# Six of twelve modulation weight tiles: multiplied by TensorE in column quarters instead of by VectorE

## The chip, the cores and the metric

The kernel runs on one core of one Trainium2 chip, in one launch. The metric is device time in microseconds (us). TensorE (PE) multiplies and writes only to PSUM; VectorE (DVE) and ScalarE (ACT) do elementwise work and may read PSUM; GpSimd (POOL) does some elementwise work and issues indirect gathers; SyncE (SP) issues the large weight transfers. The engines run side by side and meet only at semaphores.

## The reference, cut to what matters

256 tokens of width 1024 pass through two transformer-like blocks. The first block is modulated by a condition vector c, and this is the part that the change touches:

```
c_act = silu(c)                                    # (1, 1024)
mod = (c_act @ ada_w + ada_b)[:, None, :]          # (1, 6144)
sh1, sc1, gt1, sh2, sc2, gt2 = split(mod, 6)
h = rms_norm(x, g) * (1 + sc1) + sh1
p = h @ w_in                                       # four mixers (rwkv7, spatial gating, short conv, S5) and gates
x = x + gt1 * (merged @ w_o)
h = rms_norm(x, g2) * (1 + sc2) + sh2
x = x + gt2 * (square(relu(h @ ffn_w1)) @ ffn_w2)
```

The second block has two attentions and a layer that gathers 128 expert rows for each token from a table in HBM. Everything is float32.

## The kernel before, in words

**The modulation.** `ada_w` is 1024 x 6144. It arrives as twelve tiles, ada 0 to 11, of 128 partitions x 4096 values (2 MB): eight chunks k of 128 input rows lie side by side, each 512 output columns wide. Tiles 0 to 3 make sh1 and sc1, which the first product needs; 4 and 5 make gt1; 6 to 9 make sh2 and sc2; 10 and 11 make gt2.

In VectorE's `ada_sum(i)` each of 128 partitions multiplies its eight chunks by its eight values of c_act (columns 0 to 7 of `cact`) and adds them up: two TENSOR_SCALAR (line 1177), six SCALAR_TENSOR_TENSOR (line 1180) into two accumulators, and one TENSOR_TENSOR that adds the two (line 1183). The result, 128 x 512, lies in `mrow[:, i % 2, :]`. The sum over the 128 partitions is left to TensorE: `mod_gt(i)` (line 547) multiplies `mrow` by a matrix of ones, `mod_T(i)` (line 540) multiplies by one column of ones, to have the result as a column. VectorE then adds the bias. Tile 2 is already shared: VectorE takes half of its chunks, TensorE the others with one column of c as weights (line 558).

**The order of the work.** Each engine's program is written out by hand, as a Python function per engine. For the mixers, all of them walk through the same generator, `mixer_order()`: projections, then a plan of gate tiles and modulation tiles. It is `PLAN = [gates 4, ada 4, gates 5, gates 2, ada 5, gates 3, bc 0, gates 6, gates 7, ada 6, gates 0, ada 7, gates 1]`, and ada 8 is put in the middle of gates 1. Between the halves of a gate product stand steps of the mixers' own chains (a table `SCHEDULE` of the letters a, b, c, d). So in a gate tile's time TensorE alternates four instructions of the gate (`gate`, line 613, eight in the profile) with short products of the rwkv7 chain "a" and the S5 chain "d" (mostly through a helper, line 517). VectorE's S5 levels are lines 1444 and 1451, its part of the rwkv chain lines 1525 to 1548. When the walk yields "ada", only VectorE does something; when it yields "mod", TensorE and VectorE do.

**Ada 9** stands behind the walk. On VectorE it is between the end of chain "d" and the end of chain "a"; TensorE's `mod_T(9)` stands behind `merge(0)`, ahead of the products `glu(1, 0)`, `glu(1, 1)` and `w_o`.

**The ring.** SyncE loads the tiles in one order (`STREAM`) into a ring of three places. A load waits until the tile that lay in its place is spent: for a tile of TensorE that is the semaphore of the bank with its last product, for an ada tile VectorE's count `ada_taken`. The place of ada 9 is next given to the first tile of `w_o`; that of ada 4 to ada 5, of ada 5 to o_c.

**PSUM.** Eight banks. Names from the pool "misc" take banks 4, 5, 6 in turn; to take a bank TensorE waits until its last content was drained.

Of the kernel before, what the change touches and what calls it, by code (L numbers as in the profile page):

```python
# [14 lines left out]
P = 128  # L15
# [261 lines left out]
def build(nc, A, out):  # L277
    with ExitStack() as ctx:
# [19 lines left out]
        cact = sb("cact", [P, 16])  # L298
        wf = sb("wf", [P, 8, 8])
# [188 lines left out]
        spent = {("ada", i): (sig("ada_taken"), i + 1 if i < 2 else i) for i in range(12) if i != 2}  # L488

        def summed(i):  # L490

            return sig("ada"), i + 1 if i < 2 else i
# [5 lines left out]
        def tensor():  # L498
# [49 lines left out]


# [276 lines left out]
            for what, arg in mixer_order():  # L826
                if what == "p":
                    project(*arg)
                elif what == "gate":
                    gate(*arg)  # L830
                elif what == "merge":
                    merge(*arg)
                elif what == "mod":
                    mod_gt(arg[0]) if arg[0] < 6 else mod_T(arg[0])
                elif what == "step":
                    next(branch[arg[0]], None)
                elif what == "rest":
                    for _ in branch[arg[0]]:
                        pass
# [33 lines left out]
            merge(0, "misc")  # L873
            mod_T(9)
# [260 lines left out]
        def vector():  # L1135
# [98 lines left out]
            tell(v.tensor_tensor(cact[:, 0:8], cols[:, C_C:C_C + 8], cact[:, 8:16], ALU.mult), "c_times")  # L1234
            after()
# [6 lines left out]
            ada_sum(2)  # L1242
            mod_T(0, 0)
# [358 lines left out]
            for what, arg in mixer_order():  # L1602
                if what == "p":
                    project(*arg)
                elif what == "merge":
                    merge(*arg)
                elif what == "ada":
                    ada_sum(*arg)
                elif what == "mod":
                    mod_gt(arg[0], 0, arg[0] - 4) if arg[0] < 6 else mod_T(arg[0], 4 * arg[0] - 8)  # L1610
                elif what == "step":
                    next(branch[arg[0]], None)
                elif what == "rest":
                    for _ in branch[arg[0]]:
                        pass
# [3 lines left out]
            ada_sum(9)  # L1619
# [354 lines left out]
        def scalar():  # L1974
# [221 lines left out]

            branch = {"a": rwkv(), "b": gating(), "c": iter(()), "d": s5()}
            for what, arg in mixer_order():
                if what == "p":
                    project(*arg)  # L2200
                elif what == "gate":
                    gate(*arg)
                elif what == "step":
# [19 lines left out]
            evacuate("zA", f4(zA))  # L2223
            glu(1, 0)
# [469 lines left out]
```

## Time and profile before

| what | us |
|---|---|
| median of 3 runs | 1472.91 (1471.83 to 1474.8) |
| span of the profiled execution, first to last instruction | 1467.3 |
| median less that span (what lies around it) | 5.6 |
| PE busy in the span | 1211.4 (83%) |
| DVE busy | 942.2 (64%) |
| ACT busy | 397.3 (27%) |
| POOL busy | 374.9 (26%) |

The profiled execution has its span and no total of its own, so the total is taken as the span and 5.6 us. The profile's page shows one execution. Its strips cut the span in 40 slices of 36.7 us; a digit is the busy share in tenths. Matmuls overlap, so the duration of one (601 ns for 128x512) is longer than the distance between the starts of two; the length of a group of many is the better measure. A float32 product of the code appears as two MATMUL rows, each with its weight load (PEld): "x8" in the profile is four products of the code.

### The profile page before, as it was taken

How to read it: one execution, taken by the hardware profiler on the slowest of the kernel's cores; microseconds unless marked ns; L12 is line 12 of the kernel's file. 1: busy time of each engine (PE TensorE's matmuls, PEld its weight loads, DVE VectorE, ACT ScalarE, POOL GpSimd, SP SyncE). 2: the span in 40 equal slices, each digit the busy share in tenths (PEclk: the TensorE clock that was granted, in tenths of full speed). 3: DMA queues.
4: the chain of work that ended last, by engine and by line, in shares of the span. 5: the costliest groups of instructions: out<-in, count | busy, mean ns of one | idle time of the engine just before them, and what ended most of it. 6: DMA issues, size and time to landing. Idle time of an engine off the chain costs nothing.

```text
span 1467.3 us, 14350 instructions
## 1 busy us (share of the span) xinstructions
PE 1211.4 (83%) x4968; PEld 748.5 (51%) x4968; DVE 942.2 (64%) x2039; ACT 397.3 (27%) x1051; POOL 374.9 (26%) x285
## 2 busy tenths in 40 slices
PE   4989999999999999888787377668589887787776
PEld 3875655664767775487553265333473333232322
DVE  6288877973210231175866799996788776776654
ACT  2242111131101222122201223333234333333323
POOL 0001211201000000022533243432358444444420
PEclk9999999999999999999989699988799999999999
DMA  9733434465896667479999999999999999999996
GB/s 396 270 122 129 140 129 176 173 229 229 293 358 280 239 235 245 177 321 424 423 424 423 423 422 421 425 421 422 384 400 421 420 421 420 421 420 421 420 421 265
DMA packets 56376, 484.31 MB, mean 330 GB/s; under 512 B 6512, under 2 KB 8816, under 8 KB 10224
## 3 DMA queue, kind: packets, MB, share of 16 engines
q0 software_dynamic: 36864, 268.45, 44.2%
q1 hardware_dynamic: 18288, 211.35, 36.9%
q10 hardware_dynamic: 1152, 3.59, 0.6%
q8 instruction: 39, 0.64, 0.2%
q14 instruction: 33, 0.27, 0.1%
HBM read 482.33 MB, written 1.05 MB: 329 GB/s over the span
## 4 chain that ended last, share of the span: by engine, by line
PE 45%; DMA 28%; DVE 19%; issue 4%; ACT 3%; POOL 0%; DVEq 0%; SPq 0%; ACTq 0%
PE ps L517 23%; DMA ring<-in_euv,arena 16%; DMA arena<-in_euv,arena 7%; PE ps L613 6%; PE ps L980 6%; PE ps L904 5%; DVE xr L1910 4%; DMA ring<-in_w 3%; DVE arena L1886 3%; PE ps L1115 3%; DVE arena L1444 1%; DVE ring L1886 1%; DVE arena L1451 1%; DMA ring<-in_pq 1%; DVE arena L1180 1%
## 5 line engine op out<-in xcount | busy, mean ns | idle before, releaser
L2483 POOL DMA_INDIRECT arena<-in_euv,arena x161 | 206.1, 1280 | 575.2 <-DVE arena L1839 302.0
L517 PE MATMUL ps<-arena,ring 128*128 128x128 f32 (+1 forms) x1664 | 235.2, 305 | 28.8 <-DMA ring<-in_qkv 5.8
L517 PEld LDWEIGHTS ps<-arena,ring 128*128 128x128 f32 x1664 | 223.9, 204 | 44.4 <-issue 9.8
L1886 DVE CUSTOM_DVE_ANT_0 arena<-arena 128x1024 f32<-128x1024 f32 x161 | 195.5, 1223 | 69.9 <-DMA arena<-in_euv,arena 64.9
L517 PE MATMUL ps<-arena 128*128 128x128 f32 (+3 forms) x1276 | 178.9, 295 | 35.9 <-ACT arena L1999 23.0
L1115 PE MATMUL ps<-arena 128*128 128x512 f32 x356 | 173.5, 634 | 38.9 <-ACT arena L2355 38.5
L517 PEld LDWEIGHTS ps<-arena 128*128 128x128 f32 x1276 | 161.2, 194 | 65.5 <-issue 59.2
L2379 ACT ACTIVATE arena<-arena 128x2 f32<-128x2 f32 x127 | 25.7, 203 | 451.2 <-DVE arena L1886 450.7
L1115 PEld LDWEIGHTS ps<-arena 128*128 128x128 f32 x356 | 69.4, 201 | 139.7 <-issue 79.1
L980 PE MATMUL ps<-ring,arena 128*128 128x512 f32 x240 | 115.5, 639 | 25.0 <-DMA ring<-in_w 25.0
L1115 PE MATMUL ps<-ring,arena 128*128 128x512 f32 x216 | 103.7, 620 | 33.8 <-ACT arena L2355 33.8
L2483 POOL DMA_INDIRECT ring<-in_euv,arena x75 | 96.1, 1282 | 108.1 <-PE ps L1115 51.9
L1886 DVE CUSTOM_DVE_ANT_0 ring<-ring,arena 128x1024 f32<-128x1024 f32 x75 | 91.2, 1223 | 44.1 <-DMA ring<-in_euv,arena 43.8
L613 PE MATMUL ps<-ring,arena 128*128 128x512 f32 x256 | 116.5, 601 | 0.0
L1910 DVE SCALAR_TENSOR_TENSOR xr<-arena,xr 128x1024 f32<-128x1024 f32 x72 | 92.4, 1283 | 26.2 <-ACT arena L2382 21.9
L517 PE MATMUL ps<-ring,arena 128*128 128x512 f32 (+1 forms) x224 | 96.9, 586 | 9.9 <-DMA ring<-in_ba 4.6
L904 PE MATMUL ps<-ring,arena 128*128 128x512 f32 x192 | 93.5, 638 | 4.5 <-DMA ring<-in_qkv 3.1
L980 PEld LDWEIGHTS ps<-ring,arena 128*128 128x128 f32 x240 | 48.2, 205 | 84.6 <-issue 57.8
L1115 PEld LDWEIGHTS ps<-ring,arena 128*128 128x128 f32 x216 | 40.6, 196 | 94.7 <-ACT arena L2355 51.5
L1999 ACT COPY arena<-ps 128x512 f32<-128x512 f32 (+2 forms) x75 | 36.5, 489 | 162.2 <-PE ps L517 122.2
L613 PEld LDWEIGHTS ps<-ring,arena 128*128 128x128 f32 x256 | 47.6, 192 | 49.4 <-issue 49.0
L517 PEld LDWEIGHTS ps<-ring,arena 128*128 128x128 f32 x224 | 43.1, 198 | 56.6 <-issue 45.8
(345 smaller groups left out, 1299.7 us busy)
## 6 DMA issues: line engine op xcount, KB each, us to landing
ring<-in_w SPq DMA_DIRECT2D x24, 2048.0 KB, 11.0
ring<-in_qkv SPq DMA_DIRECT2D x9, 2048.0 KB, 12.2
ring<-in_ada SPq DMA_DIRECT2D x8, 2048.0 KB, 7.9
ring<-in_gates SPq DMA_DIRECT2D x8, 2048.0 KB, 8.0
arena<-in_w SPq DMA_DIRECT2D x6, 2048.0 KB, 11.1
ring<-in_g SPq DMA_DIRECT2D x6, 2048.0 KB, 9.7
ring<-in_pq SPq DMA_DIRECT2D x6, 2048.0 KB, 12.2
ring<-in_wp SPq DMA_DIRECT2D x5, 2048.0 KB, 8.9
```

Of the source, the lines that this page charges most:

```text
L517: ins = te.matmul(o, l, r, start=(i == 0), stop=(i == len(pairs) - 1))
L613: ins = te.matmul(psum(name)[:], hT[:, k, tt * 128:(tt + 1) * 128], w[:, k * 512:(k + 1) * 512], start=(k == 0), stop=(k == 7))
L904: ins = te.matmul(psum(name)[:], hL[tt][:, k, :], w[:, k * 512:(k + 1) * 512], start=(k == 0), stop=(k == 7))
L980: ins = te.matmul(o[:], squared[:, c, :], w[:, c * D + hf * 512:c * D + hf * 512 + 512], start=(i == 0 and c == 0), stop=(i == 7 and c == 3))
L1115: ins = te.matmul(psum(name)[:], diag[:, added[0] % N_DIAG, :], slots[slot_of[n]][:, D + hf * 512:D + (hf + 1) * 512], start=(tt == 0 and ...
L1180: ins = v.scalar_tensor_tensor(a, wk, ck, a, ALU.mult, ALU.add)
L1444: first[(i, q)] = done(v.scalar_tensor_tensor(dst[:, i, q, s_:S], src[:, i, q, 0:m], pr_[:, q:q + 1], src[:, i, q, s_:S], ALU.mult, ALU.add))
L1886: ins = v.tensor_tensor_reduce(out=x, in0=x, in1=xn[:, tt, :], scale=1.0, scalar=0.0, op0=ALU.mult, op1=ALU.add, accum_out=hv[:, n % 16:n ...
L1910: added[tt] = slot_done[n] = done(v.scalar_tensor_tensor(xs, slots[slot_of[n]][:, D:2 * D], av[:, n % 32:n % 32 + 1], xs, ALU.mult, ALU.add))
L1999: emptied(sc.copy(dst, psum(name)[:, 0:width]), name)
L2379: done(sc.activation(gl, hv[:, n % 16:n % 16 + GROUP], ACT.Gelu))
L2483: gp.indirect_dma_start(slots[i], None, A["euv"], bass.IndirectOffsetOnAxis(ap=idx[:, n // 16 % 4, e % 16:e % 16 + 1].bitcast(U32), axis=0 ...
```

## The change

Modulation tiles 4 to 9 are no longer summed by VectorE. TensorE multiplies them itself in a new function `ada_rows`, called where the walk yields "ada" (tiles 4 to 8) and behind `merge(0)` (tile 9). Its weights are `c32`, 128 x 8 x 32, zero except column 0 of each group of 32, which is c_act's chunk k. Product k goes to PSUM partitions 32 (k mod 4) to 32 (k mod 4) + 31, that is, to one of four column quarters of the array, each over 512 columns; products 4 to 7 add to 0 to 3. The 128 partitions of the bank then hold four partial sums in rows 0, 32, 64, 96 and zeros elsewhere. ScalarE copies the bank to `mrow`, and `mod_gt` / `mod_T` sum over the partitions as before. `mod` now waits for ScalarE's copy (`summed`), and SyncE's reload of the place waits for TensorE's last product (`spent`).

VectorE fills `c32` with zeros at the start and copies c_act into it behind `ada_sum(2)`. The scratch for the indirect gathers' descriptors shrinks to 8192 bytes of a partition. `SCHEDULE`, `PLAN` and the stream's order are unchanged.

```diff
+        c32 = sb("c32", [P, 8, 32])
...
-        spent = {("ada", i): (sig("ada_taken"), i + 1 if i < 2 else i) for i in range(12) if i != 2}
+        BY_TENSOR = range(4, 10)
+        nth = {i: n for n, i in enumerate((0, 1, 3, 10, 11))}
+        spent = {("ada", i): (sig("ada_taken"), nth[i] + 1) for i in nth}
 
         def summed(i):
-            return sig("ada"), i + 1 if i < 2 else i
+            return empty(f"av{i}") if i in BY_TENSOR else (sig("ada"), nth[i] + 1)
...
+            def ada_rows(i, pool="misc"):                  # TensorE
+                w = weights("ada", i)
+                if i == 4:
+                    te.wait_ge(sig("c_spread"), 1)
+                te.wait_ge(*loaded("ada", i))
+                o = take(f"av{i}", pool)
+                for k in range(8):
+                    q = 32 * (k % 4)
+                    ins = te.matmul(o[q:q + 32, :], c32[:, k, :], w[:, k * 512:(k + 1) * 512], start=(k < 4),
+                                    stop=(k >= 4))
+                ins.then_inc(*fill(f"av{i}"))
+                spent[("ada", i)] = full(f"av{i}")
...
+                elif what == "ada":
+                    ada_rows(*arg)
...
             merge(0, "misc")
+            ada_rows(9)
             mod_T(9)
...
+            done(v.memset(c32[:], 0.0))                    # VectorE
...
             ada_sum(2)
+            tell(v.tensor_copy(c32[:, :, 0:1], cact[:, 0:8].unsqueeze(2)), "c_spread")
...
-                elif what == "ada":
-                    ada_sum(*arg)
...
-            ada_sum(9)
...
+            def ada_rows(i):                               # ScalarE
+                sc.wait_ge(*full(f"mod{i - 2}"))
+                evacuate(f"av{i}", mrow[:, i % 2, :])
...
-    nc = _bacc.Bacc("TRN2", target_bir_lowering=False, num_devices=1)
+    nc = _bacc.Bacc("TRN2", target_bir_lowering=False, num_devices=1, dynamic_dma_scratch_size=8192)
```

What this does to the order is shown at three places. An "x4" here counts products of the code; ps0 to ps7 are the banks. First TensorE around tile 4, between gates 4 (line 613) and gates 5; before:

```order
L613 MATMUL ps0<-ring,arena 128x512 x4
L517 MATMUL ps6<-arena 128x128 x4
L517 MATMUL ps4<-arena 128x128 x4
L517 MATMUL ps5<-arena 128x128 x4
L517 MATMUL ps6<-arena 128x128 x4
L517 MATMUL ps3<-arena 128x256 x4
L613 MATMUL ps1<-ring,arena 128x512 x4
L749 MATMUL ps4<-K,arena 128x128 x4
```

In the changed kernel line 520 is the helper of line 517, and line 630 the gate's 613:

```order
L630 MATMUL ps0<-ring,arena 128x512 x4
L520 MATMUL ps6<-arena 128x128 x4
L520 MATMUL ps4<-arena 128x128 x4
L520 MATMUL ps5<-arena 128x128 x4
L520 MATMUL ps6<-arena 128x128 x4
L520 MATMUL ps3<-arena 128x256 x4
L562 MATMUL ps4<-ring,c32 32x512 x8
L630 MATMUL ps1<-ring,arena 128x512 x4
L766 MATMUL ps5<-K,arena 128x128 x4
```

The eight quarter products stand in TensorE's queue ahead of gates 5, and every later name of the pool moves on by a bank. Next VectorE around tile 5, among the S5 levels; before:

```order
L1444 SCALAR_TENSOR_TENSOR arena<-arena 128x192 x4
L1451 SCALAR_TENSOR_TENSOR arena<-arena 128x192 x4
L1177 TENSOR_SCALAR arena<-ring,cact 128x512 x2
L1180 SCALAR_TENSOR_TENSOR arena<-ring,cact,arena 128x512 x6
L1183 TENSOR_TENSOR arena<-arena 128x512
L1444 SCALAR_TENSOR_TENSOR arena<-arena 128x128 x4
L1451 SCALAR_TENSOR_TENSOR arena<-arena 128x128 x4
L1542 TENSOR_TENSOR arena<-arena,ps4 128x512
```

In the changed kernel lines 1444, 1451 and 1542 are 1466, 1473 and 1564:

```order
L1466 SCALAR_TENSOR_TENSOR arena<-arena 128x192 x4
L1473 SCALAR_TENSOR_TENSOR arena<-arena 128x192 x4
L1466 SCALAR_TENSOR_TENSOR arena<-arena 128x128 x4
L1473 SCALAR_TENSOR_TENSOR arena<-arena 128x128 x4
L1564 TENSOR_TENSOR arena<-arena,ps6 128x512
```

The nine instructions are gone from between two levels. Last, TensorE around tile 9, behind `merge(0)` (its four pairs of 128x512 products); before:

```order
L517 MATMUL ps6<-ring,arena 128x512 x2
L517 MATMUL ps7<-ring,arena 128x512 x2
L540 MATMUL ps4<-ones,arena 128x1 x4
L517 MATMUL ps1<-ring,arena 128x512 x2
L517 MATMUL ps2<-ring,arena 128x512 x2
```

And in the changed kernel, where line 543 is `mod_T`:

```order
L520 MATMUL ps7<-ring,arena 128x512 x2
L520 MATMUL ps4<-ring,arena 128x512 x2
L562 MATMUL ps5<-ring,c32 32x512 x8
L543 MATMUL ps6<-ones,arena 128x1 x4
L520 MATMUL ps1<-ring,arena 128x512 x2
L520 MATMUL ps2<-ring,arena 128x512 x2
```

Here `mod_T(9)` stands right behind the products whose copy it waits for.

## Rows read from the trace of the kernel before

**Rows 1.** The page: the span in 40 slices, busy tenths and GB/s.
```profile
PE   4989999999999999888787377668589887787776
DVE  6288877973210231175866799996788776776654
DMA  9733434465896667479999999999999999999996
```
**Rows 2.** The chain of waits, by start: us from the start, us, what.
```profile
181.64 3.99 DVE arena L1180 x6
...
657.88 12.94 DMA ring<-in_w
```
**Rows 3.** Windows: us, then busy of PE, PEld, DVE, ACT, POOL, PEclk, DMA, GB/s.
```profile
130.00:310.00 180.00, 174.59 (x726) 105.93 (x726) 147.53 (x317) 36.14 (x78) 36.32 (x20) 0.99 0.46 165
310.00:600.00 290.00, 283.83 (x1416) 190.55 (x1414) 75.46 (x161) 55.86 (x136) 5.06 (x4) 0.99 0.68 256
740.00:1100.00 360.00, 249.17 (x1100) 166.08 (x1099) 300.64 (x547) 103.76 (x278) 130.00 (x91) 0.86 1.00 416
```
**Rows 4.** Waits of PE from 130 to 310: us in total, times, longest.
```profile
PE ps L517 <- DVE arena L1281: 2.0, 2, 1.7
PE ps L517 <- DVE arena L1451: 1.8, 2, 1.4
PE ps L517 <- ACT arena L1999: 1.4, 2, 0.7
```
**Rows 5.** Timeline of PE: start, length, line, operation, form, count [idle before <-releaser].
```profile
140.79 3.59 PE L613 MATMUL ps<-ring,arena 128*128 128x512 f32 x8
144.22 0.60 PE L749 MATMUL ps<-K,arena 128*128 128x128 f32 x4
...
189.47 1.97 PE L517 MATMUL ps<-arena 128*128 128x256 f32 x8 [0.45 <-DVE arena L1451]
...
279.47 2.05 PE L517 MATMUL ps<-arena 128*128 128x128 f32 x16 [0.73 <-ACT arena L1999]
```
**Rows 6.** Groups of instructions by form, VectorE, 140 to 320.
```profile
L1180 DVE SCALAR_TENSOR_TENSOR arena<-ring,cact,arena 128x512 f32<-128x512 f32 x36 | 24.3, 745 | 0.0
L1177 DVE TENSOR_SCALAR arena<-ring,cact 128x512 f32<-128x512 f32 x12 | 6.0, 543 | 0.0
L1183 DVE TENSOR_TENSOR arena<-arena 128x512 f32<-128x512 f32 x6 | 5.7, 950 | 0.2
```
**Rows 7.** Timeline of PE, the start of the program.
```profile
26.99 1.02 PE L561 MATMUL ps<-arena,ones 128*1 128x512 f32 x2
27.94 1.97 PE L571 MATMUL ps<-K,arena 128*128 128x128 f32 x16
```
**Rows 8.** Timeline of DVE: before ada 0's sum, and a later wait for PE.
```profile
9.18 0.88 DVE L1177 TENSOR_SCALAR arena<-ring,cact 128x512 f32<-128x512 f32 x2 [5.86 <-DMA ring<-in_ada]
...
200.20 0.69 DVE L1542 TENSOR_TENSOR arena<-arena,ps 128x512 f32<-128x512 f32 x1 [3.56 <-PE ps L517]
```
**Rows 9.** Timeline of PE behind merge(0): mod_T(9), glu, transposes, glu and w_o.
```profile
335.94 0.95 PE L540 MATMUL ps<-ones,arena 128*128 128x1 f32 x8
336.75 3.68 PE L517 MATMUL ps<-ring,arena 128*128 128x512 f32 x8
340.26 1.04 PE L533 MATMUL ps<-K,arena 128*128 128x128 f32 x8
341.13 17.33 PE L517 MATMUL ps<-ring,arena 128*128 128x512 f32 x40
```
**Rows 10.** Timeline of SP's transfers, then median us to landing (290 to 350).
```profile
316.45 20.01 SPq L2543 DMA_DIRECT2D ring<-in_w_o  x2
...
ring<-in_w_o SPq DMA_DIRECT2D x2, 2048.0 KB, 7.8
ring<-in_w SPq DMA_DIRECT2D x1, 2048.0 KB, 14.1
```
**Rows 11.** DMA issues from 750 to 1460: KB each where one size, median us to landing.
```profile
arena<-in_euv,arena POOLq DMA_INDIRECT x140, 33.3
```

More of the change, by code:

```diff
@@ L2202, in scalar @@
                     gate(*arg)
+                elif what == "ada":
+                    ada_rows(*arg)
                 elif what == "step":
@@ L2223, in scalar @@
             evacuate("zA", f4(zA))
+            ada_rows(9)
             glu(1, 0)
```

## The prediction, on record before the changed kernel ran

> **What bounds the kernel now.** I read the slices first. TensorE is at nine tenths, once at eight, in every slice from the second through the sixteenth (to 587 us), while the DMA engines mostly stand at 3 to 8; from the nineteenth (660 us) the DMA engines are at nine tenths until the end [rows 1]. So there are two parts: up to some 620 us the kernel waits for TensorE, and behind that for HBM traffic at 416 GB/s [rows 3]. The second part cannot start earlier than the first lets it: its first tiles and gathers need ring places and results that TensorE gives, and its first big piece on the chain of waits is a weight tile from 657.88 [rows 2]. The bytes behind that point do not change. A shift of TensorE's program before 600 us therefore moves the end by as much.
>
> The changed tiles lie between 130 and 340 us. There TensorE is busy 174.59 of 180 us, at a granted clock of 0.99 (the upper level, 2.4 GHz), and from 310 to 600 us 283.83 of 290; VectorE has 147.53 of the 180 [rows 3]. Both look full, so I ask who waits for whom. In those 180 us TensorE's matmuls wait 3.8 us for VectorE and 1.4 us for ScalarE [rows 4]. That is all that a lighter VectorE could give back. The chain does show VectorE's sum of tile 5, 3.99 us from 181.64 [rows 2], but TensorE kept working through that stretch and waited only 0.45 us behind it, at 189.47 [rows 5]; VectorE itself later waits 3.56 us for TensorE, at 200.20 [rows 8]. The bound is TensorE, and the change puts work on it.
>
> **What VectorE loses.** Six tiles, nine instructions each: 24.3 + 6.0 + 5.7 = 36.0 us [rows 6]. Of the waits of TensorE only the one at 189.47 has a removed sum in the stretch ahead of it. The other three, two for line 1281 and one for line 1451, come after VectorE had waited for TensorE at 200.20 and before it reaches ada 6, so no removed sum reaches them; behind ada 6 to 8 TensorE waits for no VectorE up to 310. Value taken: -0.4 us; bounds 0 and -5.2, all of rows 4.
>
> **What TensorE gains.** Eight products per tile, each 512 columns wide. A product of float32 is two MATMUL instructions: four of the gate are "x8", and start 3.43 us before the next thing does (140.79 to 144.22), so one instruction takes 0.43 us and one product 0.86 [rows 5]. A narrow stationary side makes it no cheaper: the product with one column of weights, line 561, has its successor 0.95 us behind it (26.99 to 27.94) [rows 7]. So the sixteen instructions of a tile cost 16 x 0.43 = 6.88 us if they go one behind the other, and 1.72 us if the four quarters run wholly side by side. No row shows two quarters at once. These are the two ends.
>
> I take a value between them, from how the work is issued. The two instructions of a product use the same quarter, so the second must follow the first. TensorE takes its queue in order, and the next product's first instruction stands behind this one's second. If quarters can overlap but starts keep their order, the second half of product k runs beside the first half of product k+1, and so on: starts at 0, 1, 1, 2, 2, ... 7, 7, 8 steps, the end at 9 steps: 9 x 0.43 = 3.87 us per tile. Six tiles: 23.2 us, all of it on the bounding engine.
>
> The Trainium skill, "TensorE: Matmul & The Clock Gate", Part 3, says that matmuls start and end strictly in program order, which is the premise of that count; no run here shows it for quarters.
>
> **Changing the shape of the array.** Between the one-column product (two instructions from 26.99, so 27.85) and the full transposes at 27.94 there is 0.09 us [rows 7]. With two changes per tile I take 0.1 us per tile, 0.6 us together; bounds 0 and 1.2. The Trainium skill speaks against this edit here: "TensorEngine Tiling (Array Packing)", Key Properties, says that a change of mode drains the engine. It gives no figure; a drain of the 0.16 us by which a matmul's record overlaps the next (3.59 - 3.43) would make 12 x 0.16 = 1.9 us in place of 0.6, as an estimate, and the 0.09 us row speaks for the smaller.
>
> **ScalarE.** Six copies of 128x512 from PSUM. Five have a gate's time before `mod` needs them, and TensorE has other work: 0. For tile 9, `mod_T(9)` is the next thing in TensorE's queue, so TensorE stands while ScalarE copies, and behind it stand `glu(1,0)` and all else. Such a wait for a ScalarE copy took 0.73 us at 279.47 [rows 5]: +0.7 us (bounds 0.7 and 1.5, if ScalarE is late).
>
> **Tile 9's place in the ring.** VectorE was done with ada 9 at 316.45, and the first tile of w_o was asked for at once [rows 10]. Now its place is free only behind `merge(0)`, which ended at 335.94, and the quarter products. The load lands 7.8 us after issue with 0.33 us of SyncE, 8.1 us. TensorE needs it after the copy's wait 0.7, mod_T 0.8 (335.94 to 336.75), glu 3.5 (to 340.26), transposes 0.9 (to 341.13), glu 3.4: 9.3 us [rows 9, 10]. It is just in time, by 1.2 us: cost 0. But the second w_o tile and the first of the next stage are now asked for in the same moment; a tile in such company took 14.1 us [rows 10], and then TensorE would wait 5.1 us. I keep 0 to 5.1 and take 0, since the first in the queue has the least company.
>
> **The rest.** `c32` is cleared while VectorE waits 5.86 us for ada 0 [rows 8]; its filling is one short copy. If the first had no cover it would cost some 0.2 us. Taken: 0. The smaller descriptor scratch: the trace has 33.3 us from a gather's issue to its landing [rows 11]; at 128 rows of 2048 float32 each, 1.05 MB, and 416 GB/s (2.5 us) that is some 13 in flight. Should only half of that remain, the DMA engines still have several MB queued, so 0; if each of 256 gathers left a hole of 0.1 us, +26. No row shows it, and I leave that end out of the likeliest case's own range. The later bank numbers of the pool move by one; 0, within 1 us either way.
>
> **The sum.** Span 1467.3 + 23.2 + 0.6 + 0.7 - 0.4 = 1491.4; with the 5.6 us around the span 1497.0, against 1467.3 + 5.6 = 1472.9, the median before. The likeliest case's own range is 1492 to 1502.
>
> **Rivals.**
> *Quarters fully side by side.* 1.72 us per tile: 10.3 + 0.9 for the other terms = +11.2, 1484.1. For it: the quarters share neither array columns nor PSUM partitions. Against it: each product is two instructions on one quarter [rows 5]. The Trainium skill, "TensorE: Matmul & The Clock Gate", Part 3, "Measured speedup vs the span model", gives 3.07 times for four strips of rows and 2.38 for three of columns. By 3.07 a tile would be 2.24 us and the time 1487.2, as an estimate; no run here shows it. Chance 0.24.
> *One behind the other.* 6.88 us per tile: 41.3 + 0.9 = +42.2, 1515.1. For it: every 512-column instruction of the trace holds the engine 0.43 us, whatever its width [rows 5, 7]. Against it: only that the quarters are separate. Chance 0.26.
> *VectorE was the bound.* Then its 36.0 us come back in part: the S5 levels and rwkv steps run earlier, TensorE's short products stand ready, and records that look busy were stretched by waits. Place: the chain from 174 to 189 us. With half of it back and quarters side by side: 1472.9 + 11.2 - 18 = 1466. It decides only from 11 us given back, and rows 4 offer 5.2. For it: 147.53 of 180 us and the chain's piece at 181.64. Against it: TensorE's products follow each other at full rate, 3.43 us for eight. Chance 0.05.
> *No change.* The extra products fall wholly in waits of TensorE. There are 5.4 us of idle in 180 [rows 3], and even side by side five tiles need 8.6. Chance 0.04.
> The forecast has the rest, 0.41.
>
> **How the numbers follow.** A measurement of this kernel tells about 0.2%, 2.9 us, from no change. Faster is the third rival, 0.05; same 0.04; slower 0.91: the forecast and the first two rivals. The range must take in 1484.1 and 1515.1 besides the forecast to leave out less than 2 in 10: 1482 to 1517, the ends moved out by the 2 us of the unknown small terms.
>
> **What the profile would show.** The distance from the first quarter product of a tile to the gate's next product: 1.7, 3.9 or 6.9 us, that alone tells the first three cases apart. VectorE's busy time falls by 36 us less 0.3. Waits of TensorE for VectorE between 130 and 310 stay at 3 to 4 us. At `mod_T(9)` TensorE waits 0.7 us for ScalarE; at the first `w_o` product it doesn't wait for DMA. From 660 us on all is as before, shifted. I am wrong if TensorE's time from gates 4 to gates 1 doesn't grow by five tiles' price, or if the part behind 660 us takes another length: then look at the gathers.

## The result, and the profile after

The changed kernel takes 1481.85 us (median of 4 runs, 1481.15 to 1483.14) against 1472.39 us of the kernel before on the same chip (1471.83 to 1474.8): ratio 1.0055 [1.0039, 1.0071], so some 6 to 10 us slower. The forecast was 1497.0 with a range from 1482 to 1517. The direction was right; the rise was forecast 2.5 times too large (24.1 us against 9.5), and the time lies just below the range. One later execution of the kernel before took 1807.89 us at a granted clock of 0.65; it is slow and left out of all comparisons.

The profiled execution took 1481.15 us, its span 1479.9. First the timeline of TensorE around tiles 4 and 5 after the change, against [rows 5] (start, length, line, operation, form, count; "..." marks lines left out):

```profile
138.23 5.47 PE L520 MATMUL ps<-arena 128*128 128x128 f32 x40
143.63 1.92 PE L562 MATMUL ps<-ring,c 128*32 128x512 f32 x16
145.48 3.70 PE L630 MATMUL ps<-ring,arena 128*128 128x512 f32 x8
149.02 0.60 PE L766 MATMUL ps<-K,arena 128*128 128x128 f32 x4
...
185.10 1.92 PE L562 MATMUL ps<-ring,c 128*32 128x512 f32 x16
186.96 7.13 PE L630 MATMUL ps<-ring,arena 128*128 128x512 f32 x16
193.93 1.28 PE L520 MATMUL ps<-arena 128*128 128x128 f32 x10
```

Line 562 is the quarter products. The next thing starts 1.85 us behind the first of them (143.63 to 145.48), where the forecast said 3.87 and its first rival 1.72. The gate behind it takes 3.54 us until the next start (145.48 to 149.02), 0.11 more than the 3.43 of [rows 5]. So from the start of the quarter products a tile costs 1.96 us. It also costs 0.09 us ahead of them: the forty transposes from 138.23 take 5.40 us to the next start, and 5.31 before the change. That is 2.05 us per tile in all. Two lines of the kernel before, for this and for what follows:

```profile
135.48 5.47 PE L517 MATMUL ps<-arena 128*128 128x128 f32 x40
...
285.18 1.13 PE L517 MATMUL ps<-arena 128*128 128x128 f32 x8 [0.22 <-issue]
```

The wait of 0.45 us at 189.47 is gone: the entry at 193.93 has none. The one of 0.22 us at 285.18 is gone too. With the slower start of the products behind them, the two had cost 0.67 and 0.45 us, 1.1 in all. How the sixteen instructions of a tile lie, in two short windows, the first from 143.60 to 143.95, the second from 144.05 to 144.40:

```profile
143.63 0.64 PE L562 MATMUL ps<-ring,c 128*32 128x512 f32 x4
...
143.63 1.06 PE L562 MATMUL ps<-ring,c 128*32 128x512 f32 x8
```

Four instructions run in the first 0.35 us; eight are in the second window, since the first four end while the next four start. Groups of four follow each other by 0.43 us. The trace doesn't name the quarter of an instruction. That a group is one per quarter follows from the run below with one quarter, where instructions come 0.43 us apart and never together. So the two halves of a product don't hold back the next quarter's.

Behind `merge(0)`, against [rows 9, 10] (all engines, PEld and POOL left out):

```profile
347.86 1.92 PE L562 MATMUL ps<-ring,c 128*32 128x512 f32 x16
...
349.85 0.80 SPq L2570 DMA_DIRECT2D ring<-in_w_o  x2
349.91 0.59 ACT L2018 COPY arena<-ps 128x512 f32<-128x512 f32 x1 [9.23 <-PE ps L562]
350.54 1.05 PE L543 MATMUL ps<-ones,arena 128*128 128x1 f32 x8 [0.76 <-ACT arena L2018]
...
355.85 17.33 PE L520 MATMUL ps<-ring,arena 128*128 128x512 f32 x40
```

Tile 9's copy keeps TensorE waiting 0.76 us (forecast 0.7). `w_o`'s tiles are asked for at 349.85 and land a median of 8.0 us later (357.8):

```profile
ring<-in_w_o SPq DMA_DIRECT2D x2, 2048.0 KB, 8.0
```

The line at 355.85 holds the eight instructions of `glu(1, 1)`, 3.43 us, and then `w_o`'s, from 359.28 on, with no wait in between. The tile was there 1.4 us ahead of its use, and the two terms taken as 0 there were 0. The windows, against [rows 3], and the waits of TensorE from 130 to 345 us:

```profile
130.00:310.00 180.00, 173.16 (x753) 101.16 (x753) 116.81 (x270) 34.75 (x78) 23.11 (x20) 0.99 0.40 151
310.00:600.00 290.00, 284.47 (x1461) 192.47 (x1458) 71.73 (x156) 58.98 (x140) 5.08 (x4) 0.99 0.69 258
740.00:1100.00 360.00, 249.87 (x1097) 165.18 (x1096) 299.27 (x541) 101.08 (x269) 130.47 (x89) 0.85 1.00 418
```

```profile
PE ps L520 <- DVE arena L1532: 3.1, 1, 3.1
PE ps L520 <- ACT arena L2018: 2.2, 3, 0.8
PE ps L520 <- DVE arena L1303: 1.9, 2, 1.7
PE ps L520 <- DVE arena L1473: 1.4, 1, 1.4
```

VectorE has 31 us less in the first window (147.53 to 116.81; 34.6 in the whole span, 942.2 to 907.6), and but for the 0.45 us TensorE waits for it as before: lines 1303 and 1473 are lines 1281 and 1451 of [rows 4], 1.9 and 1.4 us. Line 1532's 3.1 us lies ahead of the changed tiles (before: 3.15 us at 129.38).

To sum up I use two marks, and so did the rest of the study. **Mark 1** is the start of what follows gate 4's transposes: tile 4's products or, without them, the gate's (140.79 before, 143.63 after). **Mark 2** is the start of `glu(1, 1)`, 3.43 us ahead of `w_o`'s first product (341.13, 355.85); some expectations below call it `w_o`'s first product. Between them lie all six tiles. The distance went from 200.34 to 212.22 us: **+11.9**. The difference of 2.84 us ahead of mark 1 has no changed tile in it, only the 0.09 us ahead of tile 4.

### The profile page after: what moved, and what is told of

It is laid out like the page before. It is cut to its first block, busy times and chain, and to the rows that moved or that the text cites. A ratio compares the mean times of both kernels' runs of the same rounds, so it can differ in the third digit from the quotient of the medians.

```text
span 1479.9 us, 14502 instructions
## 1 busy us (share of the span) xinstructions
PE 1230.5 (83%) x5064; PEld 752.7 (51%) x5064; DVE 907.6 (61%) x1987; ACT 400.1 (27%) x1057; POOL 365.5 (25%) x285
## 4 chain that ended last, share of the span: by engine, by line
PE 47%; DMA 29%; DVE 15%; issue 4%; ACT 3%; POOL 2%; DVEq 0%; SPq 0%; ACTq 0%
PE ps L520 24%; DMA ring<-in_euv,arena 18%; PE ps L630 7%; DMA arena<-in_euv,arena 6%; PE ps L1000 6%; PE ps L924 5%; DMA ring<-in_w 3%; DVE xr L1929 3%; DVE arena L1905 2%; PE ps L1135 2%; DVE arena L1466 1%; DVE ring L1905 1%; POOL arena L2510 1%; DVE arena L1473 1%; DMA ring<-in_pq 1%
## 5 line engine op out<-in xcount | busy, mean ns | idle before, releaser
L2510 POOL DMA_INDIRECT arena<-in_euv,arena x161 | 211.0, 1311 | 572.2 <-DVE arena L1858 303.1
L520 PE MATMUL ps<-arena,ring 128*128 128x128 f32 (+1 forms) x1664 | 231.0, 301 | 28.5 <-DVE arena L1237 6.5
L520 PEld LDWEIGHTS ps<-arena,ring 128*128 128x128 f32 x1664 | 220.0, 201 | 43.4 <-issue 9.9
L1000 PE MATMUL ps<-ring,arena 128*128 128x512 f32 x240 | 119.2, 656 | 28.3 <-DMA ring<-in_w 28.3
L1135 PE MATMUL ps<-ring,arena 128*128 128x512 f32 x216 | 109.4, 649 | 32.1 <-ACT arena L2382 32.1
L630 PE MATMUL ps<-ring,arena 128*128 128x512 f32 x256 | 117.0, 602 | 0.0
L1000 PEld LDWEIGHTS ps<-ring,arena 128*128 128x128 f32 x240 | 49.7, 212 | 90.2 <-issue 60.1
L924 PE MATMUL ps<-ring,arena 128*128 128x512 f32 x192 | 91.4, 626 | 4.3 <-DMA ring<-in_qkv 2.9
L1135 PEld LDWEIGHTS ps<-ring,arena 128*128 128x128 f32 x216 | 42.2, 203 | 95.0 <-ACT arena L2382 48.8
L2018 ACT COPY arena<-ps 128x512 f32<-128x512 f32 (+2 forms) x81 | 40.1, 497 | 179.1 <-PE ps L520 127.8
L630 PEld LDWEIGHTS ps<-ring,arena 128*128 128x128 f32 x256 | 47.6, 192 | 53.5 <-issue 53.1
L520 PEld LDWEIGHTS ps<-ring,arena 128*128 128x128 f32 x224 | 43.6, 200 | 57.6 <-issue 46.9
```

Source lines behind the costliest of these rows:

```text
L520: ins = te.matmul(o, l, r, start=(i == 0), stop=(i == len(pairs) - 1))
L630: ins = te.matmul(psum(name)[:], hT[:, k, tt * 128:(tt + 1) * 128], w[:, k * 512:(k + 1) * 512], start=(k == 0), stop=(k == 7))
L924: ins = te.matmul(psum(name)[:], hL[tt][:, k, :], w[:, k * 512:(k + 1) * 512], start=(k == 0), stop=(k == 7))
L1000: ins = te.matmul(o[:], squared[:, c, :], w[:, c * D + hf * 512:c * D + hf * 512 + 512], start=(i == 0 and c == 0), stop=(i == 7 and c == 3))
L1135: ins = te.matmul(psum(name)[:], diag[:, added[0] % N_DIAG, :], slots[slot_of[n]][:, D + hf * 512:D + (hf + 1) * 512], start=(tt == 0 and ...
L2018: emptied(sc.copy(dst, psum(name)[:, 0:width]), name)
```

## Experiments

**Does the order of the products matter?** Edit of the changed kernel:

```
-for k in range(8):
-    q = 32 * (k % 4)
+for n in range(8):
+    q, k = 32 * (n // 2), n // 2 + 4 * (n % 2)
```

> The changed kernel (1481.9 us) with the eight products of a tile in another order: 0, 4, 1, 5, 2, 6, 3, 7, so that all four instructions of a column quarter stand one behind the other in TensorE's queue. Theory A, each quarter works through its own instructions and a waiting one doesn't hold back those of other quarters: a tile stays at 1.85 to 1.96 us, the time at 1481.9 (within 1.5 us). Rival B, starts keep the order of the queue, or the engine can look past only an instruction or two: a quarter's four instructions take 1.72 us and the next quarter starts with the last of them, 13 steps of 0.43 = 5.6 us per tile, +3.6 x 6 = +22, so 1504; a short look ahead gives something between, 1487 to 1500. The trace tells it by the distance from the first quarter product of tile 4 to the gate's next product.

Measured: 1484.73 us (1481.16 to 1486.11), ratio to before 1.006 [1.004, 1.0081], as the changed kernel within the intervals (the median is 2.9 us above the changed kernel's, but the kernel before, measured again beside it, is 4.0 above its own too, 1476.43); marks 212.37 us apart. Timeline:

```profile
143.81 1.94 PE L562 MATMUL ps<-ring,c 128*32 128x512 f32 x16
145.68 3.70 PE L630 MATMUL ps<-ring,arena 128*128 128x512 f32 x8
```

and in the window from 143.85 to 144.10 alone:

```profile
143.81 0.66 PE L562 MATMUL ps<-ring,c 128*32 128x512 f32 x4
```

1.87 us with four instructions of a quarter in a row: 5.6 is out. Four run in the first 0.3 us. If these are of four quarters, as above, the first of the last quarter, which has twelve ahead of it in the queue, has started before the second of the first quarter. Each quarter works through its own instructions, as Theory A had it.

**Is it the quarters?** All eight products on `o[0:32, :]`.

> The changed kernel with all eight products of a tile on the first quarter (32 columns, partitions 0 to 31 of PSUM; the other 96 rows that the copy takes are not written by this tile, so the modulation is not the reference's). Theory A, each instruction holds its own quarter 0.43 us: sixteen one behind the other 6.88 us and about 0.1 us at the edges, 7.0 in place of 1.96 us per tile, +30 us over the changed kernel: 1512. Rival B, the quarters are not what makes the tile short, and narrow weights (32 columns) alone make an instruction cheaper: it stays under 1490.

Measured: 1514.82 us (1512.22 to 1516.94), ratio 1.0261 [1.0239, 1.0284], 30.1 us above the run before it on the same chip. Timeline:

```profile
143.83 7.05 PE L561 MATMUL ps<-ring,c 128*32 128x512 f32 x16
150.81 1.12 PE L629 MATMUL ps<-ring,arena 128*128 128x512 f32 x2
```

6.98 us, sixteen times 0.43 and 0.1, as Theory A had it. The four quarters are what saves 5.1 us per tile.

**What is the price made of?** `for n in range(16)` with `k = n % 8`: each product twice.

> The changed kernel with each tile's eight quarter products done twice over (the second pass starts its sums anew, the output is the same). Theory A, four more groups of 0.43 us at full overlap, the edges of the mode paid once: +1.72 us per tile, +10.3 us over the changed kernel, 1492.2. Rival B, the overlap is had only from what already waits in the queue (the sixteen instructions are there before the gate ends) and dries up when more come: up to 3.9 us for the second pass, +23, 1505. Rival C, a good part of a tile's 1.96 us is the change of mode: less than 1 us for the second pass, under 1488.

Measured: 1496.2 us (1494.69 to 1497.05), ratio 1.0137 [1.0113, 1.016], 11.5 us above the run with the pairs adjacent (Theory A: +10.3). Timeline:

```profile
146.12 3.64 PE L563 MATMUL ps<-ring,c 128*32 128x512 f32 x32
149.69 1.98 PE L631 MATMUL ps<-ring,arena 128*128 128x512 f32 x4
```

3.57 us for 32 instructions, 1.72 more than for 16: four more groups of 0.43. What is left of a tile's 1.96, 0.24 us, is paid once, as are the 0.09 us ahead of it: the edges. The overlap doesn't dry up.

**What is the relief worth?** In the kernel before:

```
+if 4 <= i <= 9:
+    tell(v.tensor_scalar(acc[0], w[:, 0:512], cact[:, 0:1], None, ALU.mult), "ada_taken")
+    after()
+    tell(v.tensor_tensor(acc[0], acc[0], acc[0], ALU.add), "ada")
+    return
```

> The kernel before (1472.4 us) with VectorE's sums of tiles 4 to 9 cut to one multiplication and one addition each (seven of nine instructions left out, some 29 of 36 us; these six sums are wrong), and nothing put on TensorE. Theory A, VectorE was no bound: only the wait of 0.45 us at 189.47 goes, 1472.0, within 0.7 us of the kernel before. Rival B, VectorE was a bound for part of the stretch: a third to half of the 29 us come back, 1458 to 1463. The trace's profile also tells whether the clock of TensorE at the program's start moves the whole kernel: the start of the first weight product (line 558) and what it takes, 5 or 6.4 us, beside the span.

Measured: 1471.85 us, ratio 0.9972 [0.9959, 0.9984], or 4.6 us. The marks stand 199.25 us apart, 1.09 less than before. Rival B (1458 to 1463) is out. The trace speaks for A and the timed runs for more. The trace also starts late: mark 1 at 146.08, 5.3 us later than before, though nothing ahead of it is changed.

**The side edits alone**, with the sums left on VectorE:

> The kernel before with the change's two side edits alone: c32 is reserved, cleared and filled (nothing reads it), and the scratch for descriptors is 8192. All sums stay on VectorE. Theory A, both cost nothing: the ratio to the kernel before is 1.000 within 0.002. Rival B, the smaller scratch slows the gathers: their landing (33.3 us in the median before) grows, and the time by more than 3 us. The profile of this run is at the same time a second sample of the program's start: after the change, and with the sums cut, line 558's eight instructions took 6.4 and 5.9 us instead of 5.05, and I expect the same here, 2 to 6 us later at 129.38, if that has nothing to do with the edits.

Measured: 1472.39 us, ratio 0.9991 [0.9976, 1.0005]. Both cost nothing. Windows of TensorE, of the kernel before and then of this one:

```profile
34.00:40.00 6.00, 6.00 (x29) 1.00 0.99 418
...
316.00:322.00 6.00, 6.00 (x21) 0.50 0.80 273
324.00:340.00 16.00, 15.28 (x45) 1.00 0.18 53
```

```profile
34.00:40.00 6.00, 5.56 (x20) 0.73 0.99 419
...
314.00:326.00 12.00, 10.92 (x45) 0.50 0.67 248
328.00:340.00 12.00, 11.28 (x30) 1.00 0.00 0
```

The column behind the counts is the granted clock. It stands at 0.50 (1.2 GHz) over the 12 us from 314 here, and over 6 us from 316 in the kernel before. The marks are 2.63 us further apart for that alone. Ahead of mark 1 the kernel before is also the quicker, 140.79 against 143.16. The execution from which I had the durations was a lucky one.

**TensorE's price without the relief:** VectorE's sums kept, ScalarE's copy waits for the sum and writes over it. A tile's place in the ring is given back behind that copy and not behind TensorE's last product. The part of the edit that matters most below:

```
+sc.wait_ge(sig("ada"), i)
 evacuate(f"av{i}", mrow[:, i % 2, :])
```

> The changed kernel, with VectorE's sums of tiles 4 to 9 kept as before beside TensorE's quarter products (ScalarE's copy waits for the sum and writes over it, the output is the same). So TensorE's price stands alone, without the relief. Theory A, relief is worth 0.5 to 1.1 us in the trace (sums cut: 1.1 us between 140 and 341 us): this kernel is 1 us slower than the changed one, ratio to before 1.008. Rival B, relief is worth what the timed medians of the cut sums say, 4.6 us (2.4 to 6.1): then this kernel stands at before + 12 to 14, ratio 1.009 to 1.0095 at least, and the trace shows more waits of TensorE between 130 and 600 us than the changed kernel has.

Measured: 1484.47 us, ratio 1.0058 [1.0035, 1.0081]; marks 212.81 apart, 0.59 above the changed kernel's. The interval is too wide to tell A from B, and the 0.59 us are not VectorE's load on TensorE. They are one wait, behind tile 6:

```profile
279.96 1.07 ACT L2021 COPY arena<-ps 128x512 f32<-128x512 f32 x2 [11.02 <-DVE arena L1203]
...
281.09 2.05 PE L520 MATMUL ps<-arena 128*128 128x128 f32 x16 [0.35 <-ACT arena L2021]
```

ScalarE stands 11.02 us for the end of VectorE's sum (line 1203), which the edit itself asks of it, and its next copy is late for TensorE. The two waits that the change took away, at 189.47 and 285.18 of the kernel before, are gone here too, with all sums in place: TensorE reaches these points 4 us and more later. Beside the quarter products the sums therefore cost nothing between the marks.

**Tile 9's place:** `ada_rows(9)` ahead of `merge(0)`.

> The changed kernel with tile 9's quarter products ahead of merge(0) in place of behind it. Nothing else moves. Theory A, tile 9 costs 1.96 us of products and about 0.76 us of TensorE standing while ScalarE copies; with the products ahead of merge(0) the copy lies beside its 3.5 us and the wait is gone: 0.8 to 0.9 us less than the changed kernel, about before + 8.6 (ratio 1.0058), and no wait for ScalarE before mod_T(9). Rival B, ScalarE is then late with zA's copy or the copy itself comes behind other work and merge(0)'s banks wait: the same time as the changed kernel, with the wait in another place.

Measured: 1482.29 us, ratio 1.0049 [1.0031, 1.0067]; marks 211.25 apart, 0.97 less. Theory A by the marks; a ratio with this interval can't show 1 us. TensorE's timeline behind the copy has no wait:

```profile
344.66 7.13 PE L520 MATMUL ps<-ring,arena 128*128 128x512 f32 x16
351.63 0.95 PE L543 MATMUL ps<-ones,arena 128*128 128x1 f32 x8
```

**Can the clock at the start be had?** 28 and 6 products of `ones` by `ones`, 128 columns, ahead of `mod_T(0)` and `mod_T(1)` of the kernel before:

> The kernel before with idle products on TensorE at the start: 28 products of 128 columns (ones by ones into a bank that nobody reads yet) before mod_T(0) and 6 before mod_T(1), while TensorE would stand and wait for VectorE's sums. Theory A, the spread of the runs and the 2.75 to 5.3 us by which the traces differ at 129.38 come from the clock that TensorE has between 20 and 40 us; kept busy from 1 us on it is at its upper level by then: line 558's eight instructions take 3.5 to 5 us, line 596's sixteen 3.7, and the time falls by 3 to 6 us against the median before (ratio 0.996 to 0.998). Rival B, the clock rises no earlier, or falls again before 33 us: no gain, ratio 1.000; or the idle products delay mod_T(0), up to 2 us slower.

Measured: 1471.92 us, ratio 0.9989 [0.9974, 1.0004]: no gain. The windows say why:

```profile
2.00:10.00 8.00, 7.75 (x54) 1.00 1.04 388
12.00:14.00 2.00, 0.00 (x0) 0.61 0.93 393
14.00:24.00 10.00, 8.36 (x31) 0.50 1.01 428
28.00:34.00 6.00, 4.42 (x35) 0.91 1.01 410
34.00:40.00 6.00, 6.00 (x15) 0.52 1.01 429
```

TensorE idled for 5.04 us behind the first products, and the clock fell; it idled again ahead of 34 (1.58 us), and the clock fell again. That is Rival B; the idle products stood in the wrong places.

**In the right places:** 7 ahead of the first projection, 13 ahead of the 128x2 products, three times 2 at the waits from 310 to 317, each inside a wait. The second of the five places:

```
 o = take("bon", "misc")
+for _ in range(13):
+    te.matmul(o[:, 0:128], ones[:], ones[:], start=True, stop=True)
 te.wait_ge(sig("rk"), 1)
```

> The kernel before with idle products on TensorE (ones by ones, 128 columns, into a bank that the next real product overwrites) only where it stands and waits: 7 ahead of the first projection (1.58 us of waiting at 33.45), 13 ahead of the 128x2 products (3.15 us at 129.38), and 2 each at three waits between 310 and 317. Theory A, the runs differ by how long the granted clock stays at 0.5 behind these three stretches of waiting (34 to 40, 129 to 140, 313 to 328 us: 3.7 to 6.4 us for line 596, 5.4 to 5.9 for line 613, 1.3 to 4 us in the third); with the waits filled the clock stays at 1.00 there, and the time falls by 3 to 8 us: ratio 0.9945 to 0.998. Rival B, the low stretches begin from something else than these waits, or the idle products come into the way: ratio 1.000 or above.

Measured: 1466.55 us (1465.59 to 1469.48) against 1476.07, ratio **0.9944 [0.9926, 0.9962]**, by the ratio some 8 us faster than the kernel before. It beats both kernels. Windows:

```profile
34.00:40.00 6.00, 6.00 (x29) 1.00 0.98 414
...
130.00:140.00 10.00, 8.74 (x49) 1.00 0.55 198
...
316.00:322.00 6.00, 6.00 (x26) 1.00 0.86 300
```

The clock is 1.00 in all three places, and the runs lie within 4 us, those of before within 13. Theory A holds. The three places were filled together, so what each is worth alone isn't shown.

**Two of them again:** the changed kernel, and the sums cut.

> The changed kernel itself once more, with more runs, on one chip with the sums cut. Theory A: before + 9.5 to 10, ratio 1.0065; its trace has the same distances as the first one between marks that lie behind each other at full clock: 164.5 us from tile 4's to tile 8's products, and a different span only by the stretches at clock 0.5. Rival B: the first ratio, 1.0055, was read against too few runs of before and the true one lies above 1.008 (12.5 us of TensorE's price, no relief).

> The kernel with VectorE's sums cut, once more (seven of nine instructions of tiles 4 to 9 left out, these sums are wrong). Its trace gave 1.1 us back between the same marks, its timed runs 4.6 us (2.4 to 6.1). Theory A, the trace is right and the rest was chance of the clock: ratio 0.9990 to 0.9995 this time, or an interval that holds 0.9993. Rival B, there is a gain that the marks of one trace don't show: ratio 0.997 again.

Measured: 1483.04 us, ratio 1.0049 [1.0031, 1.0068], which holds Theory A's 1.0065 and rules out 1.008; tile 4's to tile 8's products 164.48 us, as in the first trace. And 1470.29 us, ratio 0.9963 [0.9945, 0.998], marks 199.26 apart: Rival B's 0.997, not Theory A. So timed runs again say about 5 us for the cut sums, and the marks 1.1.

**On the quiet base.** The filled waits in four kernels: alone, with the change, with the sums cut, with both.

> The kernel before with the three waits of TensorE filled by idle products, as in the earlier run (1466.6 us there, ratio 0.9944), as the base for the next three on the same chip. Theory A: ratio 0.994 again, runs within 2 us of each other, granted clock 1.00 at 34 to 40, 129 to 140 and 310 to 330 us. Rival B: the first was luck, 0.997 or above.

> The changed kernel with the same three waits filled. Theory A, the change is six times 1.96 us of products, 0.76 us of waiting for ScalarE and 0.6 to 1.1 us of relief, and nothing of it has to do with the clock: base + 11.5, unless the transfers at the end are by now the bound: the base's part behind w_o was 3 us longer than the kernel before's, so up to 3 us of the 11.5 may be hidden there, base + 8.5 to 11.5. Rival B, the relief is worth 4 to 5 us at any clock: base + 5 to 8.

> The base with VectorE's sums of tiles 4 to 9 cut (seven of nine instructions of each left out, these sums are wrong). Theory A, relief is 0.6 to 1.1 us, the other 3 to 4 us of the timed runs came by way of the clock's low stretches, which are filled here: 0 to 1.1 us below the base, and w_o's first product 1.1 us earlier. Rival B, the relief is real at full clock: 4 to 5 us below the base, and then the trace must show it either ahead of w_o's first product or in a shorter part behind it.

> The base with the quarter products and with VectorE's sums kept as before, so TensorE's price alone. Theory A: 0.6 us above the changed kernel with filled waits. Rival B: 4 to 5 us above it.

| filled waits, and | median us | lowest to highest | to before | marks apart | span behind mark 2 |
|---|---|---|---|---|---|
| nothing | 1466.15 | 1465.46–1468.44 | 0.9957 [0.9941, 0.9973] | 197.44 | 1126.6 |
| the change | 1475.58 | 1474.83–1476.94 | 1.0023 [1.0014, 1.0033] | 209.28 | 1124.0 |
| sums cut | 1462.34 | 1461.59–1462.85 | 0.9929 [0.9914, 0.9944] | 196.32 | 1123.4 |
| both | 1477.45 | 1475.98–1478.39 | 1.003 [1.0018, 1.0041] | 209.90 | 1125.0 |

The marks give what they gave before: change +11.84, cut -1.12, both +12.46. The medians give +9.4, -3.8 and +11.3. The base's clock is 1.00 in all three places, as A said; its ratio, 0.9957, lies between A and B, with runs 3.0 us apart and not 2. The change's +9.4 is within A's range for it (8.5 to 11.5). The sums are worth 3.8 us without the products, close to B (4 to 5), and 1.9 beside them, between A and B; about 0.6 of the 1.9 is again the wait that the edit makes (0.35 us at 279.16 in this trace). What the marks don't have lies behind mark 2. The first 260.8 us of that part are the same in the traces. From some 275 us on they scatter, whatever the edit: the transfer that SyncE issues 324.7 us behind mark 2 in the base comes 4.6 us earlier in the other trace of the same kernel, and 0.8 and 6.2 us earlier in the two traces of the changed one. So the medians show that 2.4 of the change's 11.8 us are not in the total, and one trace can't say where they went.

**What does the late part hang on?**

> The base with filled waits, and the six multiply-adds of each of VectorE's sums 4 to 9 narrowed from 512 columns to 1 (511 columns of the six sums lack three quarters of their terms and are wrong). The number and order of all instructions is the base's, VectorE has 23 us less to do. Theory A, the late part hangs on the number of VectorE's instructions (42 fewer when the sums were cut): 1465.1, the base less the 1.1 us between the marks. Rival B, it hangs on VectorE's load: 1462.3 to 1463, as with the sums cut.

> The base with the sums of tiles 4, 5 and 6 cut (seven of nine instructions of each left out, these sums are wrong). The wait at 189.47 is behind tile 5, so about 1.1 us between the marks comes back here. Rival A, the late part of 2 to 3 us belongs to the number of instructions or to nothing in these tiles: some 1 to 2.5 us below the base, 1463.7 to 1465.1. Rival B, it belongs to these tiles: 1462.3.

> The base with the sums of tiles 7, 8 and 9 cut instead (seven of nine instructions of each left out, these sums are wrong). TensorE waited for none of them: 0 between the marks. Rival A: half of the late part, 1 to 1.5 us below the base, 1464.7 to 1465.2. Rival B, the late part hangs on tile 9, whose place in the ring is w_o's: 2.5 to 3 us below the base, 1463.2 to 1463.7. If neither half gives the late part and the narrowed sums do not either, it is chance of the program's placement and not relief.

Measured: narrowed 1463.87 us (marks 196.33), tiles 4 to 6 cut 1462.27 (196.32), tiles 7 to 9 cut 1464.54 (197.45). The 1.1 us between the marks belong to tiles 4 to 6, also with no instruction less. The rest against 1466.15 is 1.2, 2.8 and 1.6 us. The narrowed sums lie between the first expectation's A and B. Tiles 4 to 6 alone give as much as all six (1462.27 against 1462.34), as the second expectation's Rival B said; tiles 7 to 9 are near the third's Rival A. But the two parts add up to more than the whole, the runs with tiles 7 to 9 cut (1463.56 to 1470.51) overlap the base's, and the base was not run again beside them, where the kernel before took 1473.47 us and not 1472.19. Differences of 1 to 2 us between the two sets therefore show little. I can't name the cause: one profile each scatters as much there (1129.2 and 1126.6 us behind mark 2 for the same filled kernel). That part of the relief, 1 to 3 us, stays open.

## Why the prediction was wrong

**Bound: right.** More work on TensorE and 34.6 us less on VectorE made the kernel slower. Cutting the sums alone gives 3.8 us on the quiet base; the tiles on TensorE with the sums kept cost 11.3, about 0.6 of it a wait that this edit makes.

**The failing step: six tiles at 3.87 us.** It rested on "starts keep their order", so that a product's second half, which must wait for its own quarter, holds back the next product. The single instructions show four starting together at 143.63, and with a quarter's four instructions in a row it is 1.87 us, not 5.6. The four queues go side by side: 4 x 0.43 and an edge, 1.85. The term was 23.2 us and measured 6 x 1.85 = 11.1: 12.1 of the 15 us between forecast and result. The first rival had the mechanism, with too small a chance, 0.24; its time, 1484.1, is 2.3 us above the result. What I should have weighed: "a waiting instruction holds the queue" was my assumption, which no row bore out.

The Trainium skill's sentence, "TensorE: Matmul & The Clock Gate", Part 3, that matmuls start and end strictly in program order, does not describe this case: the run with each quarter's products adjacent shows them not held by those ahead of them (1.87 us, where program order asks for 5.6). The same part's 3.07 times for four strips of rows gave an estimate of 2.24 us; measured for four of columns is 6.98 / 1.85 = 3.8 times.

**Mode changes: too small.** 0.1 us per tile, 0.6 in all, bounds 0 and 1.2; measured 0.09 ahead of a tile, 0.11 behind it and 0.13 within its 1.85 (1.85 less 4 x 0.43), together 0.33, or 2.0 us for six. The 1.9 us that the prediction named and set aside was nearer. The one gap of 0.09 us that it took for both edges is no more than the first of them. Whether all of the 0.33 is the change of shape isn't shown.

**Tile 9's wait: right.** 0.7; measured 0.76, and 0.97 us back when the copy is covered.

**Relief: size short, cause wrong.** I took 0.4 us, the wait at 189.47, as what the removed sum gives back. Between the marks 1.1 us of waits are gone, this one and one at 285.18 that I had not priced. They are also gone where the sums are kept beside the products, so it is TensorE's own delay that fills them and not VectorE's relief. Cutting the sums without the products takes away the same 1.1. The 1 to 3 us more in the medians, whose cause is open, are in neither.

**The terms taken as 0: right.** No wait for DMA at `w_o`, 1.4 us to spare; side edits 0.9991 [0.9976, 1.0005]; the median landing of the gathers is 33.0 us after and 33.3 before [rows 11].

**Around the span: misread.** I took 5.6 us between span and median as a fixed part. The executions show about 1.3 (1481.15 less 1479.9, 1483.54 less 1482.2). By that the traced execution of before took 1468.6 us, at the low end of all its later runs (1468.31 to 1481.83). The other 4.3 are put down to luck with the clock: against the run of the side edits it is 2.4 us earlier at mark 1 and 2.6 shorter between the marks, with the clock at 1.00 from 34 to 40 (0.73 there) and low for 6 us where the other had 12. As a step from this trace to the median 5.6 happened to be the right size.

**The account.** Products 6 x 1.85 = 11.1, edges outside them 6 x 0.20 = 1.2, the wait for ScalarE 0.8 (0.76), waits filled -1.1: 12.0, less the 0.09 that lies ahead of mark 1, against 11.9 between the marks (11.84 on the quiet base). With these terms the forecast would have been 1472.9 + 12.0 = 1484.9; measured 1481.85. On the quiet base 2.4 us of the marks' 11.84 do not reach the median, which is most of the difference of 3; why, is open.

## What to carry to other kernels

Column quarters of TensorE worked independently here: price such a set of products by one quarter's own instructions (four of 0.43 us) and 0.33 us of edges per visit, in either of the two orders of issue that were run. All quarters had equal work; unequal ones were not run. Even so it is lost time where TensorE is the bound and the engine relieved is not. Before a difference of a few microseconds is explained, look at the granted clock behind each wait of TensorE; idle products put into such waits took 6 to 8 us off this kernel and made its runs comparable. An experiment that keeps old work beside new can add a wait of its own, so look at each wait before naming its price. Of an assumption on issue order, give the case without it the same weight until a row decides.

## What was not expected of the hardware

**The clock behind short waits.** Behind waits of 1.58 and 3.15 us, and two of 0.5 us among narrow products, the granted clock fell to 0.50 for a stretch, in some executions: in the kernel before it is 1.00 from 34 to 40 behind the same 1.58 us. With products just in those waits it stayed at 1.00 there; with products that ended 5 us ahead of the next real one it did not. In the stretch at 314 the 12 us of the run of the side edits stand against 6 in the kernel before, with the same TensorE program, and the marks are 2.63 us further apart.

**VectorE's sums stop GpSimd.** Timeline of GpSimd in the kernel before, during VectorE's sum of tile 5, and ahead of it:

```profile
169.18 1.09 POOL L2447 TENSOR_TENSOR arena<-arena,K 128x512 f32<-128x512 f32 x1 [7.40 <-PE ps L517]
180.45 6.12 POOL L2447 TENSOR_TENSOR arena<-arena,K 128x512 f32<-128x512 f32 x1 [10.19 <-PE ps L517]
```

The same operation takes 1.09 and 6.12 us. The ten of them have a mean of 2456 ns before and 1133 ns after the change; with tiles 4 to 6 cut 1181, with tiles 7 to 9 cut 2458. VectorE's closing addition (line 1183), at 185.65, took 1.47 us, and 0.69 for most of the others. So the sums of tiles 4 to 6 cost GpSimd 13 us (24.6 to 11.8 over the ten) that are in no account above. Between the marks the kernel doesn't show them, since TensorE was the bound; whether they have a part in the open 1 to 3 us was not tested.

The Trainium skill, "SBUF — State Buffer", Terms, says that VectorE and GpSimd share a pair of ports, locked for a whole instruction, and that the loser blocks. The trace agrees in that the two slow each other, 6.12 us against 1.09, and here GpSimd's one instruction lasted through most of a sum of nine of VectorE's. That the ports are the reason no run here separates from another.
